# A two-block transformer kernel on one core: modulation loads placed in PE's order of use, and the four branches mixed chunk by chunk into the output projection's first unit

## What is computed

```
# block 1, each of 2 layers
h = rmsnorm(x, g_mix); proj = h @ w_in            # 1024 -> 6656; 4096 columns are gate inputs
y_a..y_d = conv, neighbourhood attn, dilated attn, window attn     # 4 branches, 256 wide
branch[n] = y_n @ w_branch[n]                     # 256 -> 1024
mixed = sum_n sigmoid(gate_pre[n] + gate_b[n]) * branch[n]
x = x + mixed @ w_out                             # 1024 -> 1024
x = x + conv_ffn(rmsnorm(x, g_ffn))
# block 2, layer l
m = silu(cond) @ w_mod[l] + b_mod[l]              # 1024 -> 9216, for c and c_ctx
```

## Time and profile before

| | |
|---|---|
| median of 3 runs | 2856.56 us (2851.97 to 2856.76) |
| the profiled execution, its own time | 2862.43 us |
| its span in the trace | 2860.6 us |
| PE busy | 2633.6 us, 92% |
| DVE, ACT, POOL busy | 1476.4, 1037.4, 71.1 us |
| mean granted PE clock | 0.965 |
| HBM read | 391.16 MB, 137 GB/s over the span |

### The profile page before, as it was taken

The page is one execution under the profiler, slowest core; times in us unless marked ns, Lnnn a source line. Parts: engine busy times, 40 slices in busy tenths (PEclk is TensorE's granted clock), DMA queues, the critical chain, the costliest instruction groups (busy, mean ns, idle before and its releaser), DMA issues.

```text
span 2860.6 us, 47515 instructions
## 1 busy us (share of the span) xinstructions
PE 2633.6 (92%) x19887; PEld 2299.1 (80%) x19887; DVE 1476.4 (52%) x2139; ACT 1037.4 (36%) x1403; POOL 71.1 (2%) x97
## 2 busy tenths in 40 slices
PE   6988799998979999999999899999999999888998
PEld 5878799887878987888877577888878888777998
DVE  5664677676557755333443435333353333545655
ACT  4434355443435643222233333222232222344333
POOL 3000200100020000000000000000000000000000
PEclk9999899999989999999999899999999999999999
DMA  7468455746855563243333662243232332447473
GB/s 202 134 192 254 128 159 150 212 133 206 236 161 164 167 172 95 76 117 89 95 87 91 207 193 76 78 119 94 85 94 85 112 96 76 117 108 230 137 199 96
DMA packets 613718, 394.81 MB, mean 138 GB/s; under 512 B 47819, under 2 KB 609671, under 8 KB 613285
## 3 DMA queue, kind: packets, MB, share of 16 engines
q1 hardware_dynamic: 609552, 383.03, 46.0%
q0 software_dynamic: 2960, 7.75, 1.1%
q10 hardware_dynamic: 1029, 1.47, 0.1%
HBM read 391.16 MB, written 1.05 MB: 137 GB/s over the span
## 4 chain that ended last, share of the span: by engine, by line
PE 83%; DVE 6%; ACT 4%; issue 3%; DMA 3%; DVEq 1%; ACTq 0%; POOL 0%
PE acc L890 11%; PE acc L892 10%; PE acc L891 10%; PE scores L890 6%; PE scores L892 6%; PE scores L891 6%; DVE wlo L1770 3%; PE acc L930 3%; PE acc L932 3%; PE scores L932 3%; PE scores L931 3%; PE scores L930 3%; PE acc L931 3%; DMA raw<-in_w_mod_dram 3%; ACT whi L1315 2%
## 5 line engine op out<-in xcount | busy, mean ns | idle before, releaser
L1315 ACT ACTIVATE whi<-raw 128x2048 fp32r<-128x2048 f32 (+2 forms) x336 | 567.5, 1690 | 882.2 <-PE acc L892 241.1
L1770 DVE TENSOR_TENSOR wlo<-raw,whi 128x2048 fp32r<-128x2048 f32 (+2 forms) x315 | 651.8, 2070 | 329.3 <-ACT whi L1315 328.5
L890 PE MATMUL acc<-h_hi,whi 128*128 128x256 f32 (+1 forms) x2116 | 689.2, 326 | 33.9 <-DVE h_lo L2100 12.4
L891 PE MATMUL acc<-h_lo,whi 128*128 128x256 f32 (+1 forms) x2116 | 676.8, 320 | 0.0
L892 PE MATMUL acc<-h_hi,wlo 128*128 128x256 f32 (+1 forms) x2116 | 676.3, 320 | 0.0
L890 PEld LDWEIGHTS acc<-h_hi,whi 128*128 128x128 f32 x2116 | 407.4, 193 | 74.7 <-DVE h_lo L2100 12.9
L891 PEld LDWEIGHTS acc<-h_lo,whi 128*128 128x128 f32 x2116 | 407.5, 193 | 29.1 <-issue 1.7
L892 PEld LDWEIGHTS acc<-h_hi,wlo 128*128 128x128 f32 x2116 | 406.8, 192 | 27.2
L890 PE MATMUL scores<-h_hi,whi 128*128 128x256 f32 (+1 forms) x928 | 309.5, 333 | 0.0
L892 PE MATMUL scores<-h_hi,wlo 128*128 128x256 f32 (+1 forms) x928 | 309.3, 333 | 0.0
L891 PE MATMUL scores<-h_lo,whi 128*128 128x256 f32 (+1 forms) x928 | 309.3, 333 | 0.0
(11 more groups left out here) (293 smaller groups left out, 3468.6 us busy)
## 6 DMA issues: line engine op xcount, KB each, us to landing
raw<-in_ffn_w_in_dram SPq DMA_DIRECT2D x176, 512.0 KB, 5.0
raw<-in_w_mod_dram SPq DMA_DIRECT2D x72, 1024.0 KB, 5.9
raw<-in_w_in_dram SPq DMA_DIRECT2D x62, 1024.0 KB, 5.6
raw<-in_w_up_dram SPq DMA_DIRECT2D x88, 512.0 KB, 4.7
raw<-in_ffn_w_out_dram SPq DMA_DIRECT2D x64, 704.0 KB, 4.6
raw<-in_w_down_dram SPq DMA_DIRECT2D x32, 704.0 KB, 4.7
raw<-in_w_out_dram SPq DMA_DIRECT2D x16, 1024.0 KB, 6.0
raw<-in_w_branch_dram SPq DMA_DIRECT2D x16, 512.0 KB, 10.0
```

The lines of the kernel that those rows point to most:

```text
L890: pe.matmul(bank, wh, hi[:, c0 + k, 0:width], start=(k == 0), stop=False)
L891: pe.matmul(bank, wh, lo[:, c0 + k, 0:width], start=False, stop=False)
L1315: return act.activation(out_, in_, ACT.Copy, **kw)
L1770: dve.tensor_tensor(wlo[:, s % 2, 0:el], raw[:, slot, 0:el], f32(whi[:, s % 2, 0:el]), ALU.subtract).then_inc(s_lo, 1)
```

## The change

It has three parts. First, `mod_order` puts each modulation unit behind the gate unit that follows its place in PE's order: m3 behind G4 and not behind G6, m0 to m2 all behind G3, and so on. PE's own order of gate and modulation units is not changed. Second, in the branches DVE makes the next unit's `wlo` after three gate products, not ahead of the first. Third, the last branch is joined by chunks: POOL sums its eight tiles singly (eight sums of 128 x 256 in place of two of 128 x 1024), ACT makes `h1_hi` in eight copies, DVE `h1_lo` in eight differences that alternate with the last gate products, and PE runs the first output unit chunk after chunk (both tiles of a chunk, then the next chunk), each as soon as its `h1_lo` is there.

```diff
--- before.py
+++ after.py
@@ -245,9 +245,10 @@
     given = {}
     for l in range(DEPTH):
         for k in range(len(SLOT_GATES)):
-            after = gates_block1(k)[-1] + 1
-            for u, g in zip(mods_block1(l, k), (after, after, after + 1)):
-                behind = (f"1.{l}.gates", g) if g < 16 else (f"1.{l}.branch", g - 16)
+            gates_ = gates_block1(k)
+            use = gates_ if k not in (0, 3) else []
+            for u, g in zip(mods_block1(l, k), use + [gates_[-1]] * (SLOT_MODS - len(use))):
+                behind = (f"1.{l}.gates", g + 1) if g < 15 else (f"1.{l}.branch", g - 15)
                 given.setdefault(behind, []).append((0, u))
     for l in range(DEPTH):
         given[(f"2.{l}.out", 0)] = [(1, u) for us in mods_block2(l) for u in us]
@@ -805,13 +806,18 @@
                             pool.dma_start(dst.rearrange("p (a c) -> p a c", c=GRID_W), src).then_inc(s_rpb, 16)
 
                 ph = by_name[f"1.{l}.branch"]
-                for j in range(1, BRANCHES):
+                for j in range(1, BRANCHES - 1):
                     for m in range(0, DC, 4):
                         pool.wait_ge(s_accfree, ph.t0 + DC * j + m + 4)
                         if j > 1:
-                            pool.wait_ge(s_mix, 6 * l + 2 * (j - 2) + m // 4 + 1)
+                            pool.wait_ge(s_mix, 12 * l + m // 4 + 1)
                         pool.tensor_tensor(gates[:, m:m + 4, :], gates[:, m:m + 4, :], gates[:, DC * j + m:DC * j + m + 4, :],
                                            ALU.add).then_inc(s_mix, 1)
+                pool.wait_ge(s_mix, 12 * l + 4)
+                for m in range(DC):
+                    j = BRANCHES - 1
+                    pool.wait_ge(s_accfree, ph.t0 + DC * j + m + 1)
+                    pool.tensor_tensor(gates[:, m, :], gates[:, m, :], gates[:, DC * j + m, :], ALU.add).then_inc(s_mix, 1)
 
             pool.wait_ge(s_accfree, by_name[f"1.{DEPTH - 1}.up"].t0)
             pool.dma_start(cstage[:, :, :], A["ctx_2"][0].rearrange("(t p) d -> p t d", p=P)).then_inc(s_cx, 16)
@@ -1165,8 +1171,21 @@
                         pe.wait_ge(s_olo, n("job") - len(pairs) + 2 * j)
                     unit(nm + "branch", j, None, br_hi, br_lo, SEQ,
                          lambda w, s, m, k: w[:, s, k * D + m * P:k * D + m * P + P], c0=2 * j, ring=4)
-                pe.wait_ge(s_mixlo, 2 * (l + 1))
-                for j in range(4):
+                ph = by_name[nm + "out"]
+                pe.wait_ge(s_lo, ph.s0 + 1)
+                pe.wait_ge(s_accfree, ph.t0 - 2)
+                for k in range(DC):
+                    pe.wait_ge(s_mixlo, DC * l + k + 1)
+                    for m in range(2):
+                        cols = slice(k * 256 + m * P, k * 256 + m * P + P)
+                        wh, wl = (w[:, ph.s0 % 2, cols] for w in (whi, wlo))
+                        bank = bank_of(ph, 0, m)[:, 0:SEQ]
+                        pe.matmul(bank, wh, h1_hi[:, k, :], start=(k == 0), stop=False)
+                        pe.matmul(bank, wh, h1_lo[:, k, :], start=False, stop=False)
+                        ins = pe.matmul(bank, wl, h1_hi[:, k, :], start=False, stop=(k == DC - 1))
+                        if k == DC - 1:
+                            ins.then_inc(s_acc, 1)
+                for j in range(1, 4):
                     unit(nm + "out", j, None, h1_hi, h1_lo, SEQ, plain(256))
                 norm(norm_x(1, ("g_ffn", l), h1_hi, h1_lo))
                 first_units(nm + "up", h1_hi, h1_lo, SEQ, 1)
@@ -1589,9 +1608,9 @@
                 n("job", len(pairs))
                 for j in range(BRANCHES):
                     round_next(nm + "branch", j, None)
-                for c in range(2):
-                    act.wait_ge(s_mix, 6 * l + 5 + c)
-                    copy(h1_hi[:, 4 * c:4 * c + 4, :], gates[:, 4 * c:4 * c + 4, :], scale=0.5).then_inc(s_mixhi, 1)
+                for c in range(DC):
+                    act.wait_ge(s_mix, 12 * l + 5 + c)
+                    copy(h1_hi[:, c, :], gates[:, c, :], scale=0.5).then_inc(s_mixhi, 1)
                 ph = by_name[nm + "up"]
                 spec = norm_x(1, ("g_ffn", l), h1_hi, h1_lo)
                 out_squares(nm + "out", spec)
@@ -2086,19 +2105,25 @@
                 if l == DEPTH - 1:
                     mod_finish(0, range(3))
                 n("job", len(pairs))
+                def mixed(c):
+
+                    dve.wait_ge(s_mixhi, DC * l + c + 1)
+                    dve.scalar_tensor_tensor(h1_lo[:, c, :], gates[:, c, :], 0.5, f32(h1_hi[:, c, :]),
+                                             ALU.mult, ALU.subtract).then_inc(s_mixlo, 1)
+
                 ph = by_name[nm + "branch"]
                 for j in range(BRANCHES):
-                    rest_next(nm + "branch", j, None)
                     for m in range(DC):
+                        if m == 3:
+                            rest_next(nm + "branch", j, None)
                         t = ph.t0 + DC * j + m
                         dve.wait_ge(s_acc, t + 1)
                         gate = gates[:, DC * j + m, :]
                         dve.scalar_tensor_tensor(gate, gate, 1.0, bank_of(ph, j, m, 4)[:, 0:SEQ], ALU.add, ALU.mult).then_inc(s_accfree, 1)
-                for c in range(2):
-                    dve.wait_ge(s_mixhi, 2 * l + c + 1)
-                    s = slice(4 * c, 4 * c + 4)
-                    dve.scalar_tensor_tensor(h1_lo[:, s, :], gates[:, s, :], 0.5, f32(h1_hi[:, s, :]),
-                                             ALU.mult, ALU.subtract).then_inc(s_mixlo, 1)
+                        if j == BRANCHES - 1 and m >= 3:
+                            mixed(m - 3)
+                for c in range(DC - 3, DC):
+                    mixed(c)
                 ph = by_name[nm + "out"]
                 spec = norm_x(1, ("g_ffn", l), h1_hi, h1_lo)
                 for j in range(4):
```

## The result

The changed kernel takes 2810.48 us, the median of 4 runs (2806.56 to 2813.41), against 2856.66 us of the kernel before beside it (4 runs, 2851.97 to 2864.48). The ratio is 0.9835, 95% interval 0.981 to 0.986: faster by 46 us in the medians, or 1.65% by the ratio. The forecast was 2805.0 us in 2782 to 2833, and faster. The profiled execution took 2810.24 us at a span of 2808.5, where the one of before took 2862.4 at 2860.6.

What follows compares the result with a forecast made beforehand. PE was taken as the bound, idle for modulation loads: gates 115, branches 32 and join 32.5 make 179.5 us per layer against 207.4 and 203.2. Gain 51.6 gives 2810.8, less 5.9 for the median 2805.0, range 2782 to 2833.

Steps and rivals of the forecast that it cites:

- Gates: Gates stage of block 1: modulation load waits go, 115 us per layer, gains of 25.8 and 19.6 us.
- bounds 0 and 6: Last units of the gates stage: late loads cost 1.0 us per layer, at least 0 and at most 6.
- (a): Gates stage: DVE late with `wlo`, 1.8 us at G7 in slot 1 and 0.5 in slot 2.
- (c): Gates stage: the instruction gap of 1.2 us, seen in layer 1, stays; counted in each layer.
- Branches: Branch stretch: 22.6 us of work plus waits and 2 for the clock, 32 us; gains 3.3 and 5.4.
- its 3.0 us: First branch: B1 lands late, so gate product 3 is late and PE waits 3.0 us, bounds 0.7 to 4.5.
- Join and output: Join and output projection: 32.5 us per layer, losing 1.2 and 1.3; a shorter join would make the forecast wrong.
- The chain that the prediction named: Join: after the eighth sum come ACT copies, table load, split, DVE `wlo` and add, 12.7 us or somewhat more.
- The wait of 4 us: Join: after the first output unit PE waits 4 us, as O1's `wlo` stands at a chain's end.
- The clean run: Rival: B1 in time, sums and differences pass each other, clock kept; 167.7 us per layer, gain 75, 2781 us; chance 0.14.
- The stream: Rival: the load stream keeps its mean 225 GB/s and becomes the bound; gain 20.6, 2836 us; chance 0.14.
- gate unit pays for the new order: Rival: 24 gate units late by 2.6 us each behind modulation units cost 62.4 us, 2867 us; chance 0.06.

Runs made afterwards that it cites:

- Kernel 6: Changed kernel with DVE's copy-out of the modulation moved ahead of the softmax peaks, taps and weight remainder: 2806.59 us, ratio 0.9812.
- Kernel 1: Kernel before with only the new place of the modulation units in the load stream: 2830.69 us, ratio 0.9917.
- kernel 3: Kernel before with only the next unit's `wlo` in the branches moved behind three gate products: 2842.95 us, ratio 0.9962.
- kernel 9: The changed kernel run again, unaltered, in another group: 2810.0 us, ratio 0.9826 to the kernel before.
- kernel 7: Changed kernel with ACT's rounding of O1's weights behind the fifth copy and the table load ahead of the copies: 2803.54 us, ratio 0.9803.
- kernel 4: Changed kernel with POOL's sums of branches cut to 1 of 256 columns, so the result is wrong: 2800.94 us, ratio 0.9812.
- 10: Changed kernel with the copy-out ahead of the peaks, O1's rounding behind the fifth copy and the table load ahead of the copies: 2798.28 us, ratio 0.9786.
- 11: Kernel 10 with the `wlo` of a branch behind four gate products in place of three: 2798.68 us, ratio 0.9791.
- kernel 12: Kernel 10 with the convolution's taps shared out 6, 8, 7 in place of 4, 9, 8: 2795.4 us, ratio 0.9774.
- kernels 2: Changed kernel with the old place of the modulation units in the load stream, so branch and join parts alone: 2844.97 us, ratio 0.9966.

## Why the prediction was right, step by step

**Gates.** Forecast 115 us, measured 118.0 and 116.8. The main step holds: a modulation unit is issued long enough before its use, the loads reach 263 and 259 GB/s where the prediction asked for 255, and the 38.1 us of waits became 0.4 (forecast 1.0 a layer, bounds 0 and 6). The clock came back with them. The work is as forecast at 110.4: 118.02 less the waits of 2.5, 1.7, 3.9 and 0.4 leaves 109.5, and 116.80 less 6.4 leaves 110.4 (the parts that the prediction lists, 93.8 + 15 + 1.3, give 110.1). Two terms were too small. DVE's lateness, (a), was put at 2.3 a layer and at the `wlo` of G7 and G10. It is 4.2, and at another instruction: the copy-out behind that `wlo`, whose bank PE needs first. Kernel 6 shows both: with the copy-out moved, the waits at G7 and G10 appear, 1.37 and 0.8 us, 2.1 to 2.2 a layer and so nearly the 2.3 forecast. What the prediction left out is the copy-out in the same queue. The instruction gap, (c), was put at 1.2 for each layer, from the row of layer 1. The trace of before had another row, for the gates of layer 0:

```profile
PE stat L1057 <- issue: 3.7, 2, 2.9
```

After, it is 3.9 in layer 0, and in layer 1 2.2 with 3.3 more inside the first branch. So 2.5 of the 2.7 us missing in layer 0 stood in the trace already, and only layer 1's longer waits are new.

**Branches.** Forecast 32 us, measured 29.3 and 31.8. The waits at the eighth tile of branches 2 and 3 are 1.4 and 1.5 us in each layer (forecast 2.0 each), the one in branch 1 0.25 and 0.22 (forecast 0.3). B1 does land late: its halves take 11.2 us. But its 3.0 us show as no wait. In layer 0 the branches begin after an "issue" wait at the lower clock, so that PE arrives late itself; in layer 1 an "issue" wait of 3.3 us covers it. There gate product 3 ends at 753.26 us, 8.0 after the branches begin; PE, which by the prediction comes to the eighth tile after 4.9, would have waited the 3.0 or so that were forecast. (The work of 22.6 us isn't four times the 5.79 of a gate unit, which is 23.2. Inside a unit the matmuls of the kernel before follow each other at 0.117 us, and 192 of these are 22.4.) Kernel 1 shows the price without the move of the `wlo`: 4.83 us. The gain comes from one moved instruction (kernel 3).

**Join and output.** Forecast 32.5 us, measured 29.3 and 31.4, so in layer 0 it is shorter than before, which the prediction had named as something that would speak against it. Two terms were off. PE starts 1.5 us after the last branch matmul (forecast 2.3). The eight sums take 8.6 us together, so 1.1 each as forecast in the mean, but unevenly: the first takes 2.66, beside the last `wlo`, the later ones follow at 0.7 to 0.9, and the eighth ends 5.2 us after the last branch matmul where 5.8 was taken. In kernel 9, the same program, the join takes 30.8 us in layer 0 and 29.3 in layer 1, so which layer's is shorter is chance; against the 31.3 and 31.2 of before the mean of the four is 1.0 less. DVE from the end of the last `wlo` on, layer 1 of the changed kernel, then ACT there:

```profile
781.00 0.68 DVE L2111 SCALAR_TENSOR_TENSOR h_lo<-gates,h_hi 128x256 fp32r<-128x256 f32 x1 [0.20 <-ACT h_hi L1334]
...
786.07 2.29 DVE L1789 TENSOR_TENSOR wlo<-raw,whi 128x2048 fp32r<-128x2048 f32 x1 [2.89 <-ACT whi L1334]
788.27 0.75 DVE L2137 TENSOR_TENSOR x<-acc,x 128x256 f32<-128x256 f32 x2
```

```profile
782.30 0.42 ACT L1334 ACTIVATE h_hi<-gates 128x256 fp32r<-128x256 f32 x1 [0.46 <-POOL gates L820]
782.74 1.28 ACT L1390 ACT_TABLE_LOAD   x1
...
784.14 3.69 ACT L1334 ACTIVATE whi<-raw 128x2048 fp32r<-128x2048 f32 x2
```

The chain that the prediction named is there link by link: last copy, table load, `whi`, `wlo`, add. It ends 11.7 us after the last branch matmul, where 12.7 was forecast. PE's two starts, layer 1, then layer 0:

```profile
778.60 0.36 PE L1183 MATMUL acc<-h_hi,whi 128*128 128x256 f32 x1 [1.50 <-DVE gates L2122]
...
788.84 0.55 PE L896 MATMUL acc<-h_hi,whi 128*128 128x256 f32 x1 [4.41 <-DVE x L2137]
```

```profile
286.13 0.55 PE L1183 MATMUL acc<-h_hi,whi 128*128 128x256 f32 x1 [1.50 <-DVE gates L2122]
...
296.37 0.36 PE L896 MATMUL acc<-h_hi,whi 128*128 128x256 f32 x1 [1.79 <-DVE x L2137]
```

From the first start to the second it is 10.24 us in both layers, 788.84 - 778.60 and 296.37 - 286.13, and 10.23 and 10.22 in kernel 9. In layer 0 PE ran the first unit at the lower clock, 8.44 us, and waited 1.79; in layer 1 it ran 5.84 and waited 4.41. The chain sets the time, and a slow PE under it costs nothing. That is why kernel 7, which shortens the chain, gains as much in layer 0 as in layer 1. The wait of 4 us that the prediction took is right for layer 1 alone.

**Sum.** Forecast 179.5 a layer, measured 176.6 and 180.0. The profiled execution came out at 2810.24 against 2810.8. Its parts missed by +3.0 and +1.8 (gates), -2.7 and -0.2 (branches), -3.2 and -1.1 (join). Errors of up to 3.2 us cancel in the total, and that is luck. The 5.9 us that were then taken off for the median did not come: the changed kernel's median is that of its profiled execution, and 5.5 us above the forecast.

**Rivals.** The clean run (2781) fails on the DVE copy-out, on POOL's sums, which are worth 6 to 10 us (kernel 4), and on the "issue" waits. The stream does not become the bound, it goes at 263 GB/s. No gate unit pays for the new order: the changed kernel has no wait for a `wlo` in the six stretches, and with the copy-out moved (kernels 6, 10, 11) they are 1.37 us at G7 and 0.7 to 0.8 at G10 (0.42 and none in kernel 12).

## What to carry over

Loads in one in-order queue belong where their user stands, not in a bunch at the stage's end: that alone gave 26 of 46 us, and the clock gave part of it. What a long wait has covered becomes the next limit once it is gone: look in the queues of the other engines for every instruction that frees a buffer, the short ones too (here a copy-out of 0.55 us on DVE). Where a late transfer is feared, look at what stands behind it on the engine that waits for it: one `wlo` moved behind three products was worth 14 us. Cutting the head of a stage into chunks gains nothing while the next unit hangs on the end of the same chain; here the join became clearly shorter only once ACT made that unit's weights earlier, 26.5 to 26.8 us (with the old join that edit was not tried).

## What the runs showed of the hardware beyond this

The waits called "issue" beside B0 go with the instruction queue. DMA of the changed kernel, 251.9 to 252.3 us:

```profile
q8 instruction: 1, 0.02, 21.2%
```

One packet of instructions starts in these 0.4 us among packets of weights and takes 21.2% of 16 engines' 0.4 us, 1.36 us. By that estimate it is through by 253.3 to 253.7, and PE, which stopped with 7 of 64 matmuls of the last modulation to go, resumes at 254.96:

```profile
251.36 1.02 PE L1063 MATMUL stat<-raw,cond 128*32 128x64 f32 x57 [0.36 <-DMA raw<-in_w_mod_dram]
254.96 0.44 PE L1063 MATMUL stat<-raw,cond 128*32 128x64 f32 x7 [2.57 <-issue]
```

The other traces have the same distance. The packet starts at 274.8 us (within 0.4) in the kernel before and PE resumes at 277.84; in layer 1 of the changed kernel at 749.4 and 752.38, in kernel 1 at 254.4 and 257.30, in kernel 3, layer 1, at 788.0 and 790.92. PE resumes 2.5 to 3.1 us after the packet starts. How long it waits is then a matter of when the packet starts: in kernel 1 at least 1.8 us after PE had stopped (at 252.54), a wait of 4.76; in kernel 3, layer 1, at least 1.3 us before PE stopped (at 789.76), a wait of 1.16. That PE waits for this very packet is read from these distances and was not tried by itself.

The wait just ahead of the branches of layer 0 isn't the new order's doing. The kernel before has it at the same matmul, 2.9 us, kernels 2 and 3 with the old order 2.8 and 3.3, and the kernels with the new one 2.3 to 4.8. The changed kernel itself had 2.57 and, profiled again, 4.31. What is new is the wait in the first branch of layer 1: 2.4 to 3.4 us with the new order (kernel 1 excepted, where PE waits for a gate product at that place), 0.6 and 1.2 in kernels 2 and 3, none before. Fuller DMA queues are not seen to be the reason: the DMA share during the wait of layer 0 is 1.03 before (274.8 to 277.8 us) and 1.02 after (252.0 to 255.0). What sets the packet's start stays open.
